# Splitting an expert's weights on three engines instead of two, in a mixture-of-experts stage

## The reference, cut to what matters

```
def run_block(args):
    xb, e = args
    h = jax.nn.silu(xb @ w_gate[e]) * (xb @ w_up[e])
    return h @ w_down[e]
```

## Time and profile before

| | |
|---|---|
| median of 3 runs | 2563.74 us |
| the profiled execution's own time | 2565.68 us |
| its span, first to last instruction | 2563.5 us |
| PE busy | 2100.0 us (82%) |
| DVE busy | 1351.9 us (53%) |
| ACT busy | 1109.4 us (43%) |
| POOL busy | 450.8 us (18%) |
| mean granted clock of TensorE | 0.922 |

### The profile page before, as it was taken

The page is one execution under the profiler, slowest core; times in us unless marked ns, Lnnn a source line. Parts: engine busy times, 40 slices in busy tenths (PEclk is TensorE's granted clock), DMA queues, the critical chain, the costliest instruction groups (busy, mean ns, idle before and its releaser), DMA issues. The chain is left out here.

```text
span 2563.5 us, 40685 instructions
## 1 busy us (share of the span) xinstructions
PE 2100.0 (82%) x12292; PEld 1799.6 (70%) x12293; DVE 1351.9 (53%) x2159; ACT 1109.4 (43%) x2324; POOL 450.8 (18%) x666
## 2 busy tenths in 40 slices
PE   3999999548677788299899828999999998999950
PEld 2888888437566667299688727788888887888840
DVE  4323323237656687166222287756566557655537
ACT  3111111137555677166122116645555556555522
POOL 0111111114333445400000030000000000000026
PEclk9999999869988999699899858999999999999975
DMA  5233333493546422833323238977778869778648
GB/s 185 83 101 100 93 101 92 118 183 118 122 126 147 128 84 84 214 83 82 122 103 123 77 114 290 339 242 259 268 260 267 275 212 344 259 260 281 205 146 295
DMA packets 310794, 447.68 MB, mean 175 GB/s; under 512 B 20400, under 2 KB 212528, under 8 KB 310704
## 3 DMA queue, kind: packets, MB, share of 16 engines
q1 hardware_dynamic: 290128, 375.42, 47.8%
q0 software_dynamic: 12672, 46.14, 5.6%
q10 hardware_dynamic: 7904, 25.04, 2.4%
HBM read 330.14 MB, written 116.39 MB: 174 GB/s over the span
## 5 line engine op out<-in xcount | busy, mean ns | idle before, releaser
L575 ACT ACTIVATE prob<-score,nmax 128x512 f32<-128x512 f32 (+3 forms) x344 | 204.0, 602 | 101.5 <-DVE nmax L665 100.0
L56 PE MATMUL proj<-w_in_lo,n1T_hi 128*128 128x512 f32 (+1 forms) x640 | 244.2, 382 | 2.4 <-DVE n1T_lo L257 2.4
L58 PE MATMUL proj<-w_in_hi,n1T_hi 128*128 128x512 f32 (+1 forms) x640 | 239.1, 374 | 0.0
L57 PE MATMUL proj<-w_in_hi,n1T_lo 128*128 128x512 f32 (+1 forms) x640 | 239.1, 374 | 0.0
L58 PE MATMUL u_ps<-wu_hi,xT_hi 128*128 128x256 f32 x752 | 211.4, 281 | 0.0
L57 PE MATMUL u_ps<-wu_hi,xT_lo 128*128 128x256 f32 x752 | 211.3, 281 | 0.0
L56 PE MATMUL u_ps<-wu_lo,xT_hi 128*128 128x256 f32 x752 | 211.2, 281 | 0.0
L1687 DVE TENSOR_TENSOR wg_lo<-raw_pieces,wg_hi 128x1024 fp32r<-128x1024 f32 x124 | 147.0, 1222 | 121.7 <-ACT wg_hi L1655 119.8
L715 PE MATMUL score<-kT_lo,qT 128*128 128x512 f32 (+3 forms) x344 | 142.4, 419 | 70.6 <-ACT prob L575 42.3
L665 DVE TENSOR_REDUCE nmax<-score 128x2 f32<-128x1024 f32 (+3 forms) x172 | 171.5, 997 | 32.0 <-PE score L721 15.9
L56 PE MATMUL y_ps<-wd_lo,hT_hi 128*128 128x512 f32 x376 | 157.0, 417 | 26.7 <-DVE hT_lo L1698 26.1
(11 more groups left out here) (231 smaller groups left out, 5191.7 us busy)
## 6 DMA issues: line engine op xcount, KB each, us to landing
raw_pieces<-in_w_gate SPq DMA_DIRECT2D x128, 512.0 KB, 5.9
raw_pieces<-in_w_up SPq DMA_DIRECT2D x128, 512.0 KB, 6.9
raw_pieces<-in_w_down SPq DMA_DIRECT2D x128, 512.0 KB, 4.8
y_scratch<-zero SPq DMA_DIRECT2D x65, 512.0 KB, 2.7
qk_scratch<-qkT SPq DMA_DIRECT2D x96, 256.0 KB, 2.4
y_scratch<-y ACTq DMA_DIRECT2D x47, 512.0 KB, 6.7
x_sb<-in_x SPq DMA_DIRECT2D x32, 512.0 KB, 4.5
w_in_raw<-in_w_in SPq DMA_DIRECT2D x9, 1024.0 KB, 5.4
```

The source lines that it names most:

```text
L56: pe.matmul(out, hi, w_lo, start=first, stop=False)
L57: pe.matmul(out, lo, w_hi, start=False, stop=False)
L58: return pe.matmul(out, hi, w_hi, start=False, stop=last)
L575: act.activation(prob[:, n % RING, c, 0:w], score[:, n % 2, c, 0:w], ACT.Exp, bias=nmax[:, c, n:n + 1], accum_out=part[:, c, n:n + 1])\
```

## The change

The conversion of the pieces is dealt out by two tables. `hi` parts of pieces 0, 1 and 2 are made by DVE (a `tensor_copy`), the other nine by ACT. `lo` parts of pieces 1, 4, 7 and 9 are made by POOL, the other eight by DVE. Each engine has its own semaphore for each kind of part, and `part_ready` picks it. The copy of `y_ps` is cut in two: columns 0 to 511 by DVE, the rest by ACT. ACT takes Silu first in a replacing block. DVE now makes pieces 0 to 3 wholly before the first half of `hidden`. The small activation `warm`, which ran Silu once ahead of the experts, is gone.

```diff
+HI_BY = {k: "dve" if k < 3 else "act" for k in range(PIECES)}
+LO_BY = {k: "pool" if k in (1, 4, 7, 9) else "dve" for k in range(PIECES)}
-def part_ready(ready, e, k):
-
-    return ready, e * PIECES + (k + 1)
+def part_ready(by, ready, e, k):
+
+    own = [n for n in range(PIECES) if by[n] == by[k]]
+    return ready[by[k]], e * len(own) + (own.index(k) + 1)
...
             def _(pool):
...
+                def lows(e, first=0):
+                    for k in range(first, PIECES):
+                        if LO_BY[k] == "pool":
+                            pool.wait_ge(*hi_there(e, k))
+                            pool.tensor_tensor(piece(LO, k), raw_piece(raw, k), piece(HI, k), ALU.subtract)\
+                                .then_inc(lo_ready["pool"], 1)
+
                 def one_block(b, e, replaced):
                     gather(b + 1)
+                    if replaced:
+                        lows(e + 1)
 
                 gather(0)
+                lows(0, 8)
...
             def _(act):
...
-                    highs(0, 1, 2)
                     act.wait_ge(g_done, b + 1)
                     act.wait_ge(h_turned, b * 2 + 1)
                     act.activation(hid[:, :], g_ps[:, :], ACT.Silu).then_inc(silu_ready, 1)
-                    highs(3, 4, 5)
+                    pieces(3, 5)
                     copy_hT(b, 0)
                     copy_hT(b, 1)
                     copy_xT(b + 1)
-                    highs(6, 7, 8, 9, 10)
+                    pieces(5, 11)
                     act.wait_ge(y_done, b + 1)
                     act.wait_ge(y_stored, b * 16 + 16)
-                    act.copy(y[:, :], y_ps[:, :, :].rearrange("p a b -> p (a b)")).then_inc(y_ready, 1)
-                    act.wait_ge(y_ready, b + 2)
+                    act.copy(y[:, 512:], y_ps[:, 1, :]).then_inc(y_ready, 1)
+                    pieces(11, 12)
+                    act.wait_ge(y_ready, b * 2 + 4)
                     act.dma_start(y_d[bass.ds(b * P, P), :], y[:, :]).then_inc(y_stored, 16)
-                    highs(11)
...
-                act.wait_ge(xT_ready, 1)
-                act.activation(warm[:, :], xT_hi[:, 0, 0:1].bitcast(F32), ACT.Silu)
...
             def _(dve):
...
-                    lows(0, 1, 2)
+                    if replaced:
+                        for k in range(3):
+                            wait_used(dve, b, e, k)
+                            high(e + 1, k)
+                            low(e + 1, k)
+                    lows(3)
                     dve.wait_ge(silu_ready, b + 1)
                     hidden(b, 0)
-                    lows(3)
                     hidden(b, 1)
                     split_hT(b, 0)
                     split_hT(b, 1)
                     split_xT(b + 1)
-                    lows(4, 5, 6, 7, 8, 9, 10, 11)
+                    lows(5, 6)
+                    lows(8, 10)
+                    dve.wait_ge(y_done, b + 1)
+                    dve.wait_ge(y_stored, b * 16 + 16)
+                    dve.tensor_copy(y[:, 0:512], y_ps[:, 0, :]).then_inc(y_ready, 1)
+                    lows(11)
```

More of the change, by code:

```diff
@@ L1390, in high @@
                         act.wait_ge(raw_in[k % RAW], 16 * (k // RAW) + 16)
-                        act.copy(piece((wg[0], wu[0]), k), raw_piece(raw, k)).then_inc(hi_ready, 1)
+                        act.copy(piece((wg[0], wu[0]), k), raw_piece(raw, k)).then_inc(hi_ready[HI_BY[k]], 1)
                 act.wait_ge(step, 2)
@@ L1537, in experts @@
         y = sb("y6", [P, D])
-        warm = sb("warm6", [P, 1])
         xT_ps = ps("xT_ps", [P, KD, P])
@@ L1649, in one_block, with pieces @@
                 def one_block(b, e, replaced):
-                    def highs(*ks):
+                    def pieces(first, last):
                         if replaced:
-                            for k in ks:
+                            for k in range(first, last):
+                                if HI_BY[k] != "act":
+                                    continue
                                 wait_used(act, b, e, k)
                                 act.wait_ge(raw_in[k % RAW], e * 32 + (32 + 16 * (k // RAW) + 16))
-                                act.copy(piece(HI, k), raw_piece(raw, k)).then_inc(hi_ready, 1)
-                    highs(0, 1, 2)
+                                act.copy(piece(HI, k), raw_piece(raw, k)).then_inc(hi_ready["act"], 1)
                     act.wait_ge(g_done, b + 1)
@@ L1684, in _, with high @@
             def _(dve):
+                dve.sem_inc(y_ready, 1)
+                def high(e, k):
+                    dve.wait_ge(raw_in[k % RAW], e * 32 + (16 * (k // RAW) + 16))
+                    dve.tensor_copy(piece(HI, k), raw_piece(raw, k)).then_inc(hi_ready["dve"], 1)
                 def low(e, k):
-                    dve.wait_ge(*hi_there(e, k))
-                    dve.tensor_tensor(piece(LO, k), raw_piece(raw, k), piece(HI, k), ALU.subtract)\
-                        .then_inc(lo_ready, 1)
+                    if LO_BY[k] == "dve":
+                        dve.wait_ge(*hi_there(e, k))
+                        dve.tensor_tensor(piece(LO, k), raw_piece(raw, k), piece(HI, k), ALU.subtract)\
+                            .then_inc(lo_ready["dve"], 1)
                 def split_xT(b):
```

16 lines of the change are left out of this document (8 added, 8 removed).

## The result

The changed kernel takes 2661.51 us, the median of 4 runs (2659.4 to 2668.82), against 2562.81 for the kernel before beside it: 1.0393 times as long, interval 1.0364 to 1.0422. Slower was the likeliest case, but the forecast was 2610 and its range ended at 2636. Of the 99 us, 47 were forecast.

The account below looks back on a forecast made before the run. It took the bound in follow-on blocks to move from ACT and the transfers to DVE and POOL in turns: 2565.7 + 44 (+32 blocks, +12 clock) + 2 (gather, table loads) = 2612, 2610 against the median; range 2595 to 2628, 8-in-10 2540 to 2636.

Parts of the forecast that it names:

- Slower: Whole kernel: a longer time than before, chance 0.60, against 0.12 for the same and 0.28 for faster.
- POOL's pieces in DVE's way: Experts' follow-on blocks (replacing behind replacing): POOL's lo parts hold up DVE's, making a 17.0 us loop 24.0.
- a collision: A POOL piece beside DVE's two-input SBUF work: costs DVE 2.0 us, 3.5 times per follow-on block.
- DVE keeps the ports: Rival, experts' stage: back-to-back DVE instructions keep POOL out, transfers bound follow-on blocks at 20.7 us; 2543, chance 0.28.
- +32: Cost in the 16 follow-on blocks: 16 x 24.0 = 384 us against 352.
- other work: DVE's loop in a follow-on block without POOL's collisions: lo parts, casts, half of y, waits and registers, 17.0 us.
- cost 0 by the median: Plain blocks behind replacing ones: gather behind piece 9 lands x at 9.9 to 12.1, turned at 11.5; up to 0.6.
- my own rule: A POOL piece beside DVE's two-input SBUF operations takes 2.80 us, against 2.34 alone.
- the gather is late: Rival: piece 9 ends later, so plain blocks behind replacing ones wait 1.5 us x 15; 2635, chance 0.12 (shared with late Silu).
- the slow clock: PE's lower clock behind idle time: 1.5 us a time, paid at the end of the eight follow-on runs, +12 us.
- the table loads at 0: Experts' loops without warm: some 46 loads hidden under PE's matmuls, cost 0, with 1 us to spare behind replacing blocks.

Follow-up runs that it names:

- e1: The changed kernel with all twelve lo parts on DVE and no pieces on POOL: 2575.4 us, 1.0049 of the kernel before.
- e2: The changed kernel with the gather, for block b+2, issued between POOL's pieces 4 and 7: 2603.2 us, 1.0159 of the kernel before.
- e14: The changed kernel, POOL's pieces included, with all of SP's loads for the next expert held until x has landed: 2730.6 us, one run.
- e3: The changed kernel with warm put back ahead of the loops: 2670.8 us, 1.0417 of the kernel before.
- e12: The kernel before without warm, nothing else changed: 2580.6 us, 1.0076 of the kernel before.
- e7: The kernel before, order alone changed: Silu behind pieces 0 and 1, piece 3 behind xT: 2552.1 us, 0.9968.
- e10: The kernel before, order alone changed: Silu behind pieces 0 and 1, piece 3 between the hT copies and xT: 2533.4 us, 0.9895.
- e8: The kernel before, order alone changed: Silu behind pieces 0 and 1, piece 3 ahead of the hT copies: 2537.5 us, 0.9922.
- e13: e5 with all of SP's loads for the next expert, from piece 0 on, held until x has landed: 2703.7 us, one run.
- e4: The kernel before with POOL making the lo parts of pieces 1, 4, 7 and 9, nothing else changed: 2599.7 us, 1.0138.
- e5: e1 with the gather held until DVE has made lo part 9: 2629.5 us, 1.0266 of the kernel before.
- e11: The kernel before, order alone changed: Silu behind pieces 0 and 1, pieces 3, 4 and 5 between hT and xT: 2538.1 us, 0.9922.
- e9: e5 with SP's loads of the next expert's pieces 3, 4 and 5 held until x has landed: 2653.4 us, one run.

## Why the prediction was right and wrong

*Right in kind: POOL's pieces in DVE's way.* The routing stage's rows gave 2.0 us a collision and 2.80 for POOL's piece; the experts show 2.0 (6.41 - 2.35 = 4.06 for two) and 2.79 for `wu_lo`. "DVE keeps the ports" falls: `wd_lo` went from 1.22 to 2.56 us. The term was +32 for 24.0 us a block; measured +31.1 and 23.95. The parts were less exact than the sum: three collisions in a round instead of 3.5, and 18.2 us of other work instead of 17.0. e1 shows it for all 16 blocks. Without the pieces the forecast's own terms give 17.0 + 4 x 1.13 = 21.5 us, under the 22.0 of before, and 23.09 were measured; with them come 0.86 us more and not 2.5. So that +32 met +31.1 is luck between two errors: 17.4 of it are DVE's other work, the order and the table loads, and 13.7 the pieces.

*Wrong: the gather, "cost 0 by the median".* This is the step that failed, by 59 of the 67 us in plain blocks (e2). The time at which POOL is free for it was forecast well, with luck (piece 9 ends at 4.75, I had 4.8; but I had taken 2.3 us for a piece where my own rule gave 2.80, and the two took 2.88 and 3.39). I then added the landing of the earlier trace rows, 4.1 to 6.3, as if it were the transfer's own. It is the landing in the place where the gather stood before, 13.7 us into an isolated block, when most of the ring's loads are done. Moved behind piece 9 it goes out as SP refills the ring, and lands after 8.6. The runs separate it: 3.4 us for the loads beside it (e14 against the changed kernel, and its last plain block), 0.75 for the issue, 1.0 for the index copy, both beside DVE's `lo` parts. 15.3 against 11.5 at which x is turned gives the waits of up to 3.7 us. The rival "the gather is late" had the wait at 1.5 us a block, 2635, with a chance of 0.12, but for another reason, a late end of piece 9; measured were 4.5 us a block with piece 9 on time. Mis-sized are the landing and, behind each wait, the clock.

*Wrong by its place and size: the slow clock.* I counted 12 us on top of the follow-on blocks' 384, all at the ends of the runs, and none in plain blocks. That term isn't there: with the gather early (e2) the follow-on blocks take 382.95 in all, the clock included, and PE's busy time in the plain blocks is 2.3 us over before. With the gather late it grows by 21.0 us there, for the same matmuls. Of the 4.5 us a plain block, 2.6 are the wait for x (39.6 in 15), 1.4 the clock, and 0.4 the rest, the late `hid`. So e2 came near the forecast because the 12 us that were missing stood against 7.7 and 4.0 that I didn't have, in the plain blocks and the first.

*Wrong by a little: the table loads at 0.* I gave Silu an end between 9.3 and 10.4 us in a block behind a replacing one; it came at 11.3. DVE's half of y was on time; what I had at 1.0 us, from the store to the load, took 2.4. That used up the margin, and the 7.7 us left in e2's plain blocks are about what follows from it. Either cure would do: without the load Silu starts 1.2 us earlier and the wait for `hid` is gone (e3), and with the loads but without POOL's pieces the plain blocks are at 18.48 (e1). The gather early and no loads together weren't tried. In the kernel before the load isn't free either (e12), since Silu stands behind casts there.

*What the change's good part was worth.* Silu ahead of piece 2, with piece 3 behind xT, brings 11 us in the follow-on blocks of the kernel before (e7); with piece 3 ahead of xT it is 25 (e10), ahead of hT 32 (e8). The changed kernel spent it: even without POOL it is at 23.09, with three casts more on DVE, half of y and the table loads; which of these three costs how much there was not tried.

## What to carry to other kernels

A DMA's time from issue to landing belongs to its place and not to it: before a gather is moved, look at what the other queues have in flight at the new place, and take the landing from a gather that stands there. Work given to POOL is paid by DVE where both read two operands from SBUF: in the round shown four pieces freed 4.5 us of DVE (1.13 each) and cost it 6.1. A sum that comes out right for the stretch in view says nothing on its terms, as e1 showed, and nothing on the stretch behind it: the loss was twice as large in blocks whose own instructions the change hardly touched.

## What the runs showed of the hardware

- POOL's copy of a single index column takes 0.18 us, but 0.93 to 1.18 beside DVE's `lo` parts, and the gather's issue 1.73 instead of 0.97 (e13: POOL does nothing else there). What counts is the DVE instruction that runs when the issue starts. In e13 `lo` 11 runs already (1858.32 to 1859.54) and the issue ends 0.84 after it; in e4 the part running ends 0.3 us into the issue, which takes 1.14; in e5's follow-on blocks a cast does the same (1.07 to 1.45). Over all kernels here 229 issues began beside a running piece instruction of DVE (`hi` or `lo`), and each ended 0.84 us or more behind that one, most within 0.86; 159 began beside a running hT_lo or xT_lo, which read one operand from PSUM, and took 0.97 to 0.99. A `lo` part that starts later holds up nothing. So it is in all 62 issues of e10 and e11 with one beside them:

```profile
1728.24 0.97 POOL L1622 DMA_INDIRECT x<-n_scratch,idx  x1 [0.81 <-POOL idx L1619]
1728.69 1.23 DVE L1688 TENSOR_TENSOR wg_lo<-raw_pieces,wg_hi 128x1024 fp32r<-128x1024 f32 x1 [0.53 <-ACT wg_hi L1655]
```

- My prediction had drawn on the Trainium skill's "SBUF — State Buffer" (the "DVE blocks DMA" trap), and took only the casts to hold up the gather; a `lo` part, a TENSOR_TENSOR with two SBUF inputs, does it too. The same page infers, in "Who interferes with whom", that `tensor_tensor` leaves the writing of descriptors alone. The issues of e10 and e11 agree with that. The delayed ones show only that an issue can't begin beside a `lo` part that runs; which step of the issue waits, no run here tells.
- How the ring and the gather share the transfer engines stays open. The Trainium skill's "DMA: Bandwidth & Descriptors" (queues, rings and completion order) says that an engine takes turns between queues packet by packet. The runs show the landing growing with the bytes in flight beside it (with the longer issue taken off, 4.45 us with all loads held, some 5.9 with three, 7.3 with none, in e13, e9 and e5), but not the order in which the packets were taken.
- Leaving out a warming activation cost one table load in each loop body where Silu stood first, and two where a cast stood first (e12).
- A shorter step on one engine made isolated blocks 1.1 us longer (e3): ACT ready 1.3 us sooner put a POOL piece beside a DVE one.
